# Two blocks of 256 columns at the end of each gated feed-forward become one block of 512 columns

## The reference, cut to what matters

```python
D_FF_2 = 2816
def swiglu(u, w_in, w_out):
    a, b = jnp.split(u @ w_in, 2, axis=-1)
    return (jax.nn.silu(a) * b) @ w_out
...
    mod = jax.nn.silu(c) @ w_ada + b_ada
    sh1, sc1, g1, sh2, sc2, g2, sh3, sc3, g3 = [m[:, None, :] for m in jnp.split(mod, N_MOD, axis=-1)]
    u = rms_norm(x, ffn1_norm_g) * (1 + sc1) + sh1
    x = x + 0.5 * g1 * swiglu(u, ffn1_w_in, ffn1_w_out)
...
    u = rms_norm(x, ffn2_norm_g) * (1 + sc3) + sh3
    x = x + 0.5 * g3 * swiglu(u, ffn2_w_in, ffn2_w_out)
```

## Time and profile before

| what | value |
|---|---|
| median of 3 runs | 993.47 us (992.17 to 994.43) |
| profiled execution, span | 994.2 us |
| PE busy | 975.9 us, 98% |
| DVE busy | 715.9 us, 72% |
| ACT busy | 522.4 us, 53% |
| memory traffic | 214.64 MB, mean 216 GB/s |

### The profile page before, as it was taken

The page is one execution under the profiler, slowest core; times in us unless marked ns, Lnnn a source line. Parts: engine busy times, 40 slices in busy tenths (PEclk is TensorE's granted clock), DMA queues, the critical chain, the costliest instruction groups (busy, mean ns, idle before and its releaser), DMA issues.

```text
span 994.2 us, 12848 instructions
## 1 busy us (share of the span) xinstructions
PE 975.9 (98%) x4770; PEld 806.2 (81%) x4770; DVE 715.9 (72%) x1074; ACT 522.4 (53%) x808; POOL 58.4 (6%) x62
## 2 busy tenths in 40 slices
PE   8999999999999999999999999999999999999998
PEld 6878788888887888888878888877888878888886
DVE  5867778886786767767869988686667766566653
ACT  6576565554346444444467645567454474443531
POOL 3310100000000000000000022021000000000000
PEclk9998999999999999999999999999999999999999
DMA  7940667888795777778756766865565737664761
GB/s 245 300 132 1 222 221 226 279 271 274 264 316 192 254 262 246 247 251 325 262 149 208 229 210 190 288 194 175 150 199 199 236 111 222 215 209 134 253 225 51
DMA packets 116444, 214.64 MB, mean 216 GB/s; under 512 B 9058, under 2 KB 16506, under 8 KB 116126
## 3 DMA queue, kind: packets, MB, share of 16 engines
q1 hardware_dynamic: 116238, 213.73, 65.7%
q10 hardware_dynamic: 144, 0.10, 0.0%
HBM read 212.71 MB, written 2.13 MB: 216 GB/s over the span
## 4 chain that ended last, share of the span: by engine, by line
PE 89%; DVE 5%; DMA 2%; ACT 2%; issue 1%; POOL 0%; SPq 0%; ACTq 0%; DVEq 0%
PE ps L1179 27%; PE ps L1181 26%; PE ps L1180 26%; PE ps L1229 3%; PE ps L1316 2%; DVE wlo L1846 2%; PE ps L1271 1%; PE ps L1297 1%; PE ps L1207 1%; ACT whi L1484 1%; DMA raw<-in_w_up 1%; DMA raw<-in_w_in 1%; DMA araw<-in_w_ada 1%; DMA raw<-in_ffn_w_in 1%; PE ps L1367 1%
## 5 line engine op out<-in xcount | busy, mean ns | idle before, releaser
L1484 ACT ACTIVATE whi<-raw 128x1024 fp32r<-128x1024 f32 (+2 forms) x307 | 313.0, 1028 | 282.4 <-PE ps L1181 193.0
L1846 DVE TENSOR_TENSOR wlo<-raw,whi 128x1024 fp32r<-128x1024 f32 (+2 forms) x307 | 358.3, 1189 | 49.0 <-ACT whi L1484 48.2
L1179 PE MATMUL ps<-whi,hTh 128*128 128x512 f32 (+1 forms) x832 | 326.2, 392 | 2.7 <-DVE wlo L1846 2.7
L1181 PE MATMUL ps<-whi,hTl 128*128 128x512 f32 (+1 forms) x832 | 316.5, 380 | 0.0
L1180 PE MATMUL ps<-wlo,hTh 128*128 128x512 f32 (+1 forms) x832 | 316.4, 380 | 0.0
L1179 PEld LDWEIGHTS ps<-whi,hTh 128*128 128x128 f32 x832 | 156.8, 188 | 33.6 <-DVE wlo L1846 3.8
L1181 PEld LDWEIGHTS ps<-whi,hTl 128*128 128x128 f32 x832 | 156.7, 188 | 30.8
L1180 PEld LDWEIGHTS ps<-wlo,hTh 128*128 128x128 f32 x832 | 157.0, 189 | 26.9 <-issue 0.2
L2188 DVE SCALAR_TENSOR_TENSOR aacc<-araw,cs,aacc 128x512 f32<-128x512 f32 x126 | 94.4, 749 | 4.8 <-DMA araw<-in_w_ada 2.2
L2430 POOL TENSOR_TENSOR stat<-stat,mhalf 128x8 f32<-128x8 f32 (+3 forms) x29 | 38.3, 1331 | 632.3 <-DVE stat L1862 486.3
L1179 PE MATMUL ps<-whi,uh_ffn 128*128 128x512 f32 x176 | 69.8, 396 | 0.0
(11 more groups left out here) (251 smaller groups left out, 1092.0 us busy)
## 6 DMA issues: line engine op xcount, KB each, us to landing
raw<-in_ffn_w_in SPq DMA_DIRECT2D x80, 512.0 KB, 4.5
araw<-in_w_ada SPq DMA_DIRECT2D x72, 512.0 KB, 4.9
raw<-in_w_mix SPq DMA_DIRECT2D x64, 512.0 KB, 4.4
raw<-in_ffn_w_out SPq DMA_DIRECT2D x44, 512.0 KB, 4.9
raw<-in_w_up SPq DMA_DIRECT2D x32, 512.0 KB, 4.9
raw<-in_w_down SPq DMA_DIRECT2D x32, 512.0 KB, 5.2
raw<-in_w_out SPq DMA_DIRECT2D x16, 512.0 KB, 4.2
raw<-in_w_in SPq DMA_DIRECT2D x12, 512.0 KB, 5.6
```

The lines of the kernel that those rows point to most:

```text
L1179: pe.e.matmul(o, ah, h[:, j, :], start=s0, stop=False, skip_group_check=True)
L1181: r = pe.e.matmul(o, al, h[:, j, :], start=False, stop=s1, skip_group_check=True)
L1484: act.e.activation(uflat(whi, u), uflat(raw, u), ACT.Copy).then_inc(hi.up(u), 1)
L1846: v.tensor_tensor(uflat(wlo, u), uflat(raw, u), uflat(whi, u).bitcast(f32), SUB).then_inc(lo_dve.up(u), 1)
```

## The change

For the last i, where only 256 columns are left, the kernel no longer makes two blocks of 256 columns but one of 512, `a5`: its columns 0 to 255 are those of the activated half, 256 to 511 those of the linear half, in one pair of banks. A unit of it is loaded by two DMAs, one for each slice, each with two pieces of 256 columns for every partition. Silu reads the left half of the bank, the multiplication the right half; the pair is given back by the multiplication. The two feed-forwards have four units and eight halves less each. The planner's rules and tables are the same; it sees fewer halves.

```diff
     def ffn_blocks(m):
         for i, (c0, n) in enumerate(HB):
+            if n == 256:
+                block(f"{m}a{i}", f"{m}_w_in", 0, 8, c0, 512, m)
+                both.add(f"{m}a{i}")
+                continue
             block(f"{m}a{i}", f"{m}_w_in", 0, 8, c0, n, m)
             block(f"{m}b{i}", f"{m}_w_in", 0, 8, 2816 + c0, n, m)
...
+    def linear_of(m, i):
+        return (f"{m}a{i}", HB[i][1]) if f"{m}a{i}" in both else (f"{m}b{i}", 0)
...
                 order.append(("silu", m, i))
-                pairs.drop(f"{m}a{i}")
-                gemm(f"{m}b{i}")
-                add(f"{m}g{i}", job_glu(f"{m}g{i}", f"{m}b{i}", n))
+                if f"{m}a{i}" not in both:
+                    pairs.drop(f"{m}a{i}")
+                    gemm(f"{m}b{i}")
+                add(f"{m}g{i}", job_glu(f"{m}g{i}", linear_of(m, i)[0], n))
                 tick()
             ada_until(last_gate)
...
-    HT_FREE = {"attn": None, "mlp": "vb", "ffn1": "up7", "mix": "ffn1b5", "merged": "gb1", "ffn2": "wob1"}
+    HT_FREE = {"attn": None, "mlp": "vb", "ffn1": "up7", "mix": "ffn1a5", "merged": "gb1", "ffn2": "wob1"}
...
-                pairs.give(silu(m, i, t), f"{m}a{i}", part=t)
+                if f"{m}a{i}" not in both:
+                    pairs.give(silu(m, i, t), f"{m}a{i}", part=t)
...
+                key, c0 = linear_of(m, i)
                 dve.wait_ge(*silu(m, i, t))
-                dve.wait_ge(*ended(f"{m}b{i}", t))
-                v.tensor_tensor(b[:, 0:n], pair_of(f"{m}b{i}")[t][:, 0:n], b[:, 0:n], MUL).then_inc(glu.up(name, t), 1)
-                pairs.give(glu(name, t), f"{m}b{i}", part=t)
+                dve.wait_ge(*ended(key, t))
+                v.tensor_tensor(b[:, 0:n], pair_of(key)[t][:, c0:c0 + n], b[:, 0:n], MUL).then_inc(glu.up(name, t), 1)
+                pairs.give(glu(name, t), key, part=t)
...
+            if key in both:
+                src = d[name][0, k * 128:(k + n) * 128, :].rearrange("(k p) (s c) -> p k s c", p=128, s=2)
+                dst = uview(raw, u).rearrange("p k (s c) -> p k s c", s=2)
+                for j in range(n):
+                    r = q.dma_start(dst[:, j, :, :], src[:, j, :, c0:c0 + ncol // 2])
+                    r.then_inc(ld_raw[slot(raw, u)].up(u), 16)
+                return
```

More of the change, by code:

```diff
@@ L353, in build @@
     FFN = {"ffn1": 0, "mix": 1, "ffn2": 2}
-    blocks, units, order = {}, [], []
+    blocks, units, order, both = {}, [], [], set()
     def block(key, name, k0, nk, c0, ncol, act, a0=0, first=True, last=True, pair=None, small=0):
@@ L2535, in load_unit @@
         def load_unit(u):
-            _, name, k, n, c0, ncol = units[u]
+            key, name, k, n, c0, ncol = units[u]
             if u >= 2 * NR:
                 sp.wait_ge(*lo_dve(u - 2 * NR if u < 3 * NR else u - NR))
+            if key in both:
[5 more added lines that the diff above has]
+                return
             q.dma_start(uview(raw, u), d[name][0, k * 128:(k + n) * 128, c0:c0 + ncol].rearrange(
```

## The result

| kernel | median | executions | lowest to highest |
|---|---|---|---|
| before | 994.32 us | 9 | 991.53 to 996.85 us |
| changed | 997.73 us | 9 | 996.76 to 1001.92 us |

The account below looks back on a forecast made before the run. PE bounds the stretches the change touches. From the profiled 994.2 us: merging -1.25, moved steps -0.25, wait +3.85, clock +1.6 make 998.15 us; the span lies 0.7 above the median, so 997.4 us, range 994.2 to 999.8.

Parts of the forecast that it names:

- The merging: Both feed-forwards' input blocks: each pair of small matmuls made one large gives 0.013 us, 96 pairs 1.25 us gained.
- The rest of the merged block at nothing: In the merged block, "hi"/"lo" work, loads, and silu with the multiplication right behind a5 cost nothing.
- The wait: Ahead of ffn2's output block, PE's matmul with ones waits 3.85 us for DVE's accumulating step; bounds 2.3 and 5.5 us.
- The bias row costs nothing: At ffn2's closing step the bias row, issued before a5 ends, lands near the matmul with ones; no further PE cost.
- The clock: Behind the wait ahead of ffn2's output block the clock falls to half rate for 3.3 us, losing 1.6 us.
- the clock stays up behind it: Sign of being wrong: no clock fall behind the new wait, then 995.9 us; as a rival, chance 0.26.
- the case with the fall: Main forecast: wait ahead of ffn2's output block plus clock fall, own range 996.5 to 999.2 us, chance 0.50.
- Moved steps in the mixing part: Mixing part: a closing step leaves DVE's queue ahead of `Vm`, 0.25 us gained; bounds -0.3 to +3 us.
- No second wait in the mixing part: Rival: accumulating steps in new places make PE wait 1.5 to 3 us more there, about 999.5 us; chance 0.11.

Follow-up runs that it names:

- the kernel with the wait alone: Kernel before, unmerged, with the last two modulation steps held back to the end of ffn2's input blocks; 998.74 us, ratio 1.0032.
- the steps after the first output block: Changed kernel with the remaining modulation steps asked for only after the first output block, in both feed-forwards; 993.33 us, ratio 0.9977 to the kernel before.
- the first profile: First profiled execution of the changed kernel, nothing further changed; 996.95 us.
- the further profiles: Three more profiled executions of the changed kernel, nothing further changed; 998.65, 998.83 and 997.77 us.

## Why the prediction was right

Forecast 997.4 us, a ratio of 1.0039 to the median it was made against; measured 997.73 us and 1.0044. The terms that decide, the wait and its size, were right; that the number is so near has some luck in it, of two kinds. The forecast is the three-run median, 993.47 us, plus 3.95 us; nine executions put that median at 994.32 us, so it stood 0.85 us too low, and the measured step is 3.4 to 4.4 us. (The 0.7 us in the prediction sets a profile's span against timed executions. In all nine other profiles the span is 1.4 to 1.6 us below the time of the same execution, so the profiled execution of the kernel before was an estimated 2 us above the median. In the sum this cancels.) And the median of the changed kernel is the highest of its lower group, with nothing between 997.73 and 1000.03 us: had one of its five executions been in the upper group, the median would be 1000.03 us, above the forecast's range.

- *The merging.* Forecast 0.0130 us a pair, 0.63 us a feed-forward. Measured start to start (925.51 - 914.85) / 47 = 0.2268 us with 512 columns, as before, and 0.60 us for ffn2 in the experiment with that block alone. The Trainium skill's page "TensorE: Matmul & The Clock Gate", section "Wait — 56ns, not 53.3ns?", would give an estimated 48 x 2.5 ns = 0.12 us a feed-forward; the trace doesn't agree, with 0.60 us for these operands.
- *The rest of the merged block at nothing.* The experiment with ffn2 alone has no wait there, so loads, silu and multiplication cost nothing. In ffn1 PE has no wait from 425 to 505 us. Right.
- *The wait.* Forecast 3.85 us, released by DVE's accumulating line; 3.86 us in the timeline, and 3.89 us by the distances. The chain came link by link as it was put together from the earlier trace rows. That it is the cause was shown from both sides: taken out of the change, with all else left, the kernel is faster than before (0.9977); put into the kernel before, with nothing merged, it is slower (1.0032).
- *The bias row costs nothing.* SP issued it at 923.31, 2.4 us before a5 ended, and DVE's closing step waited for PE, not for the row. Right. In three experiments the row did come last: DVE waited for it 4.07 us in the kernel with the wait alone, where SP issued it only at 929.06 behind the loads ahead of it, 1.64 us with ffn1 alone merged, and 1.09 us with the steps after the first output block. PE didn't wait for that in any of them.
- *The clock.* Forecast: it falls, 1.6 us. It fell in three of four profiled executions and cost 1.5, 1.6 and 2.8 us; in the first profile it stayed at 1.00, and "the clock stays up behind it" was one of the prediction's own signs of being wrong. That execution took 996.95 us, inside the range given for the case with the fall, and not at 995.9 us, mostly because the median that both were built on was 0.85 us too low. So the total does not tell the two cases apart; only the further profiles do, and by them the likeliest case was rightly named, with a size that is a middle between executions rather than a number of each. The prediction also had the fall behind the wait; it began within it. That the wait brings the fall is borne out by where there is none: in the four profiles with no wait or one of 1.4 us at this place the clock is 1.00 there, and in five of the six with 3.0 us or more it falls.
- *Moved steps in the mixing part.* Forecast 0.25 us gained, from the wait at `vm1` in the earlier trace rows. That wait is gone in the changed kernel and still there, 0.3 us, in the kernel with the block merged in ffn2 alone, where these steps have not moved. From ffn1's a5 to ffn2's a5 the changed kernel takes 914.85 - 428.56 = 486.29 us in its first profile and 485.66 to 485.97 us in the three others, before 916.95 - 429.74 = 487.21 us. Of the 0.9 to 1.6 us the merging in ffn1 is 0.6, so 0.3 to 1.0 us came from the steps; two more traces in which these steps have not moved differ by 0.4 us there (486.89 and 487.26 us), so I don't read it more closely.
- *No second wait in the mixing part.* From 500 to 810 us the changed kernel waits for the same lines as before, 0.7, 1.5, 0.2, 1.8 and 0.6 us long in order of time; none is more than 0.2 us longer than its counterpart, and the one for `wlo` is gone. The rival had no part in it.

What the prediction passed over is how little it takes. In the kernel with ffn1 merged only the closing step was left over, and 1.4 us were lost, because the accumulating step ran at 925.48, late in DVE's queue; in the kernel with ffn2 merged it ran at 919.37, and nothing was lost. I had expected no wait in the first because the accumulating step stood ahead of the end of the input blocks. The queue that counts is all of DVE's, "lo"s included.

## What to carry to other kernels

Where a planner spreads side work over the main work by counting, a change that makes the main work shorter in count leaves side work over, and it is worth looking at where the rest is put: here an accumulating step of 1.53 us and the matmul behind it, at the wrong place, made PE wait 3.9 us, three times the 1.2 us that 96 matmuls less gave. Side work whose result is needed late should be asked for late; asking for it one output block later turned a loss of 0.44% into a gain of 0.23% (0.34% and 0.11% by the medians). A wait on the engine that bounds can be computed before it exists, by walking the in-order queues of the engines it waits for through a stretch of the old trace.

## What the runs showed of the hardware

- A single wait of 3.6 us in a dense stream of matmuls came with a fall of the granted clock to its lower level, 1.2 GHz, in three of four executions of one program and with none in the fourth; one of 3.0 us in another kernel and one of 5.3 us in a third came with a fall in the one execution that was profiled of each. In all five the clock fell before the wait was over, 0.1 to 2.7 us before the next matmul. The waits of 1.4 us (ffn1 alone merged, at 925.8 us) and 1.8 us (at 800 us, in every trace) were not followed by a fall; the wait of 2.3 us in attention was, in all ten traces.
- What a fall costs differs between executions of one program, 1.5, 1.6 and 2.8 us of PE's distance here.
- One 256-column matmul takes 0.1198 us from start to start and one of 512 columns 0.2266 us at the upper clock, 13 ns more than the columns at 2.4 GHz in both.
- A bias row spread to 128 partitions landed 6.9 us after its issue, and DVE used it at 7.0 us, with weight loads in flight. The page of the kernel before has 5.9 us as the median of the six such rows and 4.5 us for a weight load of 512 KB.
